# Gate products in the value tiles' PSUM banks, the value blended at eviction, and the first heads of two attentions under the value projection, in a six-layer transformer kernel

## The reference, cut to what matters

```
# layers 0 and 3 (rwkv7_time_mix)
r, k, v = xm[0] @ Wr, xm[1] @ Wk, xm[2] @ Wv
a = sigmoid(a0 + (xa @ a1) @ a2)
g = sigmoid(xg @ g1) @ g2                       # the gate
if layer == 3:                                  # the value is blended with layer 0's
    v = v + (v_first - v) * sigmoid(v0 + (xv @ v1) @ v2)
kk = normalised per head (k * k_k)
bonus = sum over a head (r * k * r_k) * v
y = scan over the tokens (r, w, k, v, kk, a)
out = ((group norm of y) + bonus) * g @ Wo
# layer 1 (stick_breaking_attention)
z = q k^T;  att = exp(log_sigmoid(z) + sum over later keys of log_sigmoid(-z));  o = att v
# layer 2 (dsa_attention)
p = softmax(q k^T / 8 over the selected keys);  o = p v
```

## Time and profile before

| what | value |
|---|---|
| three timed runs | 3889.07, 3891.84, 3902.7 us; median 3891.84 us |
| the profiled execution, its own time | 3902.21 us |
| its span, first to last instruction | 3899.5 us |
| mean granted TensorE clock | 0.982 |
| PE busy | 3746.3 us (96%) |
| POOL busy | 2632.9 us (68%) |
| ACT busy | 1880.2 us (48%) |
| DVE busy | 1612.5 us (41%) |
| transfers | 664.96 MB, mean 171 GB/s |

### The profile page before, as it was taken

One profiled execution on the slowest core, in us unless ns is written; L12 is line 12 of the kernel. 1 busy time (PEld: TensorE's weight loads), 2 busy tenths in 40 slices (PEclk: granted clock), 3 DMA queues, 4 the chain that ended last, 5 costly groups with the idle time before them and its releaser, 6 DMA issues.

```text
span 3899.5 us, 93426 instructions
## 1 busy us (share of the span) xinstructions
PE 3746.3 (96%) x36101; PEld 3562.0 (91%) x36101; DVE 1612.5 (41%) x3486; ACT 1880.2 (48%) x2746; POOL 2632.9 (68%) x1186
## 2 busy tenths in 40 slices
PE   8998998999899899899999999999999999999998
PEld 7778997998699767799999999999999999999998
DVE  6544315325532654434222375653223222266442
ACT  5325446543554432444555555455555555555643
POOL 5006873885278500288888878768888888886886
PEclk9999999998999989999999999999999999999999
DMA  6555652664356436466666646546666666664664
GB/s 186 196 202 143 183 172 76 179 184 130 87 160 191 132 112 209 146 184 189 195 193 192 191 143 186 162 136 199 191 190 194 188 186 201 185 194 129 185 182 141
DMA packets 1162954, 664.96 MB, mean 171 GB/s; under 512 B 30158, under 2 KB 1122202, under 8 KB 1162552
## 3 DMA queue, kind: packets, MB, share of 16 engines
q1 hardware_dynamic: 1162679, 661.06, 57.4%
HBM read 659.92 MB, written 1.05 MB: 170 GB/s over the span
## 4 chain that ended last, share of the span: by engine, by line
PE 43%; issue 31%; POOL 21%; DVE 3%; ACT 1%; DMA 1%; POOLq 1%; SPq 0%; DVEq 0%; ACTq 0%
PE bank L861 41%; POOL wlo L621 21%; PE bank L840 1%; DVE bank L3029 1%; POOLq L620 0%; POOLq L101 0%; ACT whi L631 0%; DMA raw<-in_w_in 0%; PE bank L961 0%; PE bank L2670 0%; PE bank L1062 0%; DVE W L1964 0%; DMA raw<-in_rw_w_rkv 0%; DVE W L1977 0%; DVE W L1962 0%
## 5 line engine op out<-in xcount | busy, mean ns | idle before, releaser
L621 POOL TENSOR_TENSOR wlo<-raw,whi 128x1024 fp32r<-128x1024 f32 (+3 forms) x1182 | 2632.7, 2245 | 1242.7 <-ACT whi L631 1238.2
L631 ACT ACTIVATE whi<-raw 128x1024 fp32r<-128x1024 f32 (+3 forms) x1182 | 1171.0, 995 | 1091.1 <-PE bank L861 915.8
L861 PE MATMUL bank<-AH,whi 128*128 128x256 f32 (+1 forms) x5712 | 1602.4, 281 | 27.4 <-DVE AL L771 9.9
L861 PE MATMUL bank<-AL,whi 128*128 128x256 f32 x5712 | 1595.1, 279 | 0.0
L861 PE MATMUL bank<-AH,wlo 128*128 128x256 f32 (+1 forms) x5712 | 1594.4, 279 | 0.0
L861 PEld LDWEIGHTS bank<-AH,whi 128*128 128x128 f32 x5712 | 1085.8, 190 | 36.4 <-issue 23.4
L861 PEld LDWEIGHTS bank<-AH,wlo 128*128 128x128 f32 x5712 | 1081.4, 189 | 0.0
L861 PEld LDWEIGHTS bank<-AL,whi 128*128 128x128 f32 x5712 | 1080.4, 189 | 0.6
L861 PE MATMUL bank<-HH,whi 128*128 128x256 f32 x1936 | 539.5, 279 | 0.0
L861 PE MATMUL bank<-HL,whi 128*128 128x256 f32 x1936 | 537.4, 278 | 0.0
L861 PE MATMUL bank<-HH,wlo 128*128 128x256 f32 x1936 | 537.4, 278 | 0.0
(11 more groups left out here) (449 smaller groups left out, 4913.6 us busy)
## 6 DMA issues: line engine op xcount, KB each, us to landing
raw<-in_ffn_w SPq DMA_DIRECT2D x420, 512.0 KB, 4.0
raw<-in_w_in SPq DMA_DIRECT2D x182, 512.0 KB, 3.9
raw<-in_ffn_w_gu SPq DMA_DIRECT2D x176, 512.0 KB, 3.8
ada_raw<-in_w_ada SPq DMA_DIRECT2D x96, 512.0 KB, 6.0
raw<-in_ffn_w_down SPq DMA_DIRECT2D x64, 512.0 KB, 3.8
raw<-in_rw_w_rkv SPq DMA_DIRECT2D x48, 512.0 KB, 3.8
raw<-in_w_ada SPq DMA_DIRECT2D x48, 512.0 KB, 5.6
raw<-in_ffn_w SPq DMA_DIRECT2D x56, 384.0 KB, 3.5
```

The lines of the kernel that those rows point to most:

```text
L621: pool.tensor_tensor(wlo[slot][:, 0:n], raw[slot][:, 0:n], whi[slot][:, 0:n], ALU.subtract).then_inc(lo_ready, 1)
L631: act.activation(whi[slot][:, 0:n], raw[slot][:, 0:n], ACT.Copy).then_inc(hi_ready, 1)
L861: mm = pe.matmul(ps[:, 0:o.shape[2]], w, o[:, k0 + c, :], start=tile not in started and c == n == 0, stop=last_panel and c == nk - 1 and n ...
```

## The change

Time mix, both layers:
- The gate products use banks 1 to 3 (`lora_banks`), the value tiles' own, in place of 4 to 7. PE no longer waits for `bonus_ready` before them but before the scan.
- The bonus product r k r_k is made on DVE right after the squares' sums, before value tile 2, and into `RW_B` (free by then), not `RW_T`. PE's bonus sums stand between value tiles 5 and 6, not behind tile 7.
- In layer 3 the value is blended as each tile is evicted (three operations of 128 x 256), and the three operations over the whole value go. Its gate (part `v`) must then be there before tile 0 is evicted. On PE its outer product stands behind value tile 0, not ahead of it.

Attentions: the first pair of heads (scores, ACT's and DVE's steps on them) is put between value tiles: after the second of four steps in `sb.v`, after the third of four in `ds.v`.

```diff
+        def lora_banks(name):
+            return bank[1:4] if name == "g" else bank[4:8]
+
         def pe_lora_out(pe, part, act_known=False):
             name = part[0]
+            banks = lora_banks(name)
...
-                if t >= 4:
+                if t >= len(banks):
                     pe.wait_ge(lora_taken, after(pe, lora_taken))
-                o, cols = bank[4 + t % 4][:, 0:S], slice(t * P, (t + 1) * P)
+                o, cols = banks[t % len(banks)][:, 0:S], slice(t * P, (t + 1) * P)
...
             if layer:
-                pe_lora(pe, parts[2])
+                pe_lora_in(pe, parts[2])
             tile(0)
+            if layer:
+                pe_lora_out(pe, parts[2])
             pe_lora_in(pe, parts[-1])
             tile(1)
...
             pe_heads(pe, const("headones"), RW_B, ready=keys_ready)
-            for s in range(2, C):
+            for s in range(2, 6):
                 tile(s)
-            pe_heads(pe, const("headones"), RW_T)
+            pe_heads(pe, const("headones"), RW_B)
+            for s in range(6, C):
+                tile(s)
             ada_round = pe_ada_start(pe, layer)
             for rnd in range(ADA_FIRST):
                 ada_round(rnd)
-            pe.wait_ge(bonus_ready, after(pe, bonus_ready))
             pe_lora_out(pe, parts[-1], act_known=True)
             pe_ada_turn(pe, bank[0], ADA_FIRST)
-            pe.wait_ge(lora_taken, after(pe, lora_taken, 4))
+            pe.wait_ge(lora_taken, after(pe, lora_taken, 3))
+            pe.wait_ge(bonus_ready, after(pe, bonus_ready))
             pe_scan(pe, layer)
...
+            def blended_value(s, j, banks):
+                o, first, ps = V[:, s * S:(s + 1) * S], VF[:, s * S:(s + 1) * S], banks[0][:, 0:S]
+                dve.tensor_tensor(o, first, ps, ALU.subtract).then_inc(dve_step, 1)
+                dve.wait_ge(dve_step, after(dve, dve_step))
+                dve.tensor_tensor(o, o, RW_XA[:, s * S:(s + 1) * S], ALU.mult).then_inc(dve_step, 1)
+                dve.wait_ge(dve_step, after(dve, dve_step))
+                dve.tensor_tensor(o, ps, o, ALU.add).then_inc(bank_free, 1)
+
+            tile = dve_tiles(dve, f"rw{layer}.v", blended_value if layer else take_copy(dve, V), by_hand=True)
+            dve.wait_ge(lora_taken, after(dve, lora_taken, 24 if layer else 16))
             tile(0)
-            dve.wait_ge(lora_taken, after(dve, lora_taken, 16))
...
+            for c in range(C):
+                cs = slice(c * S, (c + 1) * S)
+                op = dve.scalar_tensor_tensor(b[:, cs], RW_R[:, cs], vec("rw_r_k", j, c), RW_K[:, cs], ALU.mult, ALU.mult)
+            op.then_inc(head_in, 1)
+            dve.wait_ge(head_in, after(dve, head_in))
             tile(2)
             tile(3)
+            tile(4)
             dve.wait_ge(root_ready, after(dve, root_ready))
             dve.tensor_tensor(kk[:, :], kk[:, :], t[:, :], ALU.mult).then_inc(dve_step, 1)
             dve.wait_ge(dve_step, after(dve, dve_step))
-            tile(4)
...
             tile(5)
+            dve.wait_ge(head_sums, counts.at(dve, head_sums) + C // 2)
             dve.tensor_tensor(b[:, :], kk[:, :], RW_A[:, :], ALU.mult).then_inc(dve_step, 1)
...
-            if layer:
-                dve.wait_ge(head_sums, counts.at(dve, head_sums) + C // 2)
-                dve.wait_ge(lora_taken, after(dve, lora_taken, 8))
-                dve.tensor_tensor(t[:, :], VF[:, :], V[:, :], ALU.subtract).then_inc(dve_step, 1)
...
# pe_sb
+            tile = pe_panels(pe, "sb.v", fills=0, by_hand=True)
+            for st in range(G["sb.v"].steps):
+                tile(st)
+                if st == 1:
+                    pe.wait_ge(bank_free, tiles_of("sb.k"))
+                    for hd in pairs[0]:
+                        scores(hd)
             for g, pair_ in enumerate(pairs):
+                if g == 0:
+                    for hd in pair_:
+                        later(hd)
+                    pe.wait_ge(bank_free, tiles_of("sb.v"))
...
# act_sb and dve_sb: softplus(pairs[0]) and masked(hd) of the same pair behind tile(1) of sb.v
# pe_ds
+                if st == 2:
+                    pe.wait_ge(head_in, after(pe, head_in))
+                    scores(0)
+                    scores(1)
# act_ds
+                if st == 2:
+                    powers(0)
+                    powers(1)
# dve_ds
+                elif st == 2:
+                    logits(0)
+                    logits(1)
+                    weights(0)
+                    weights(1)
```

More of the change, by code:

```diff
@@ L1266, in act_lora_out @@
             dst = {"w": RW_CUM, "a": RW_A, "v": RW_XA, "g": RW_G}[name]
+            banks = lora_banks(name)
             for t in range(C):
                 act.wait_ge(lora_out, after(act, lora_out))
-                o, i = dst[:, t * S:(t + 1) * S], bank[4 + t % 4][:, 0:S]
+                o, i = dst[:, t * S:(t + 1) * S], banks[t % len(banks)][:, 0:S]
                 if name == "g":
@@ L1911, in pe_sb @@
                     pe.wait_ge(logit_ready, after(pe, logit_ready, 2))
-                for hd in pair_:
-                    later(hd)
                 if g:
+                    for hd in pair_:
+                        later(hd)
                     for hd in pairs[g - 1]:
@@ L1924, in act_sb @@
             act_norm(act, X, W[0])
-            for n in "qkv":
+            for n in "qk":
                 act_panels(act, f"sb.{n}")
@@ L1939, in softplus @@
                     act.activation(SB_SP[hd % 4], SB_SP[hd % 4], ACT.Ln, bias=1.0).then_inc(exps_ready, 1)
-            softplus(pairs[0])
+            tile = act_panels(act, "sb.v", by_hand=True)
+            for st in range(G["sb.v"].steps):
+                tile(st)
+                if st == 1:
+                    softplus(pairs[0])
             for g, pair_ in enumerate(pairs):
@@ L1989, in dve_sb @@
             pairs = [(hd, hd + 1) for hd in range(0, H, 2)]
-            for hd in pairs[0]:
-                masked(hd)
+            tile = dve_tiles(dve, "sb.v", take_tokens(dve, VT_[:, :].rearrange("p (a m) -> p a m", m=D)), by_hand=True)
+            for st in range(G["sb.v"].steps):
+                tile(st)
+                if st == 1:
+                    for hd in pairs[0]:
+                        masked(hd)
             for g, pair_ in enumerate(pairs):
@@ L2082, in pe_ds @@
                     square_sums(DS_SQ["q"])
-            tile = pe_panels(pe, "ds.v", fills=0, by_hand=True)
-            for st in range(G["ds.v"].steps):
-                tile(st)
-                if st == 0:
-                    pe_heads(pe, const("rot_head"), DS_SINE["k"])
-                if st == 1:
-                    square_sums(DS_SQ["k"])
-            pe.wait_ge(head_in, after(pe, head_in))
-            pe.wait_ge(bank_free, tiles_of("ds.v"))
             def scores(hd):
@@ L2100, in scores @@
                 mm.then_inc(ds_z_ready, 1)
+            tile = pe_panels(pe, "ds.v", fills=0, by_hand=True)
+            for st in range(G["ds.v"].steps):
+                tile(st)
+                if st == 0:
+                    pe_heads(pe, const("rot_head"), DS_SINE["k"])
+                if st == 1:
+                    square_sums(DS_SQ["k"])
+                if st == 2:
+                    pe.wait_ge(head_in, after(pe, head_in))
+                    scores(0)
+                    scores(1)
+            pe.wait_ge(bank_free, tiles_of("ds.v"))
             def turn(hd):
@@ L2169, in act_ds @@
                     inverse_norms()
-            tile = act_panels(act, "ds.v", by_hand=True)
-            for st in range(G["ds.v"].steps):
-                tile(st)
-                if st == 1:
-                    inverse_norms()
             def powers(hd):
@@ L2183, in powers @@
                 op.then_inc(exps_ready, 1)
+            tile = act_panels(act, "ds.v", by_hand=True)
+            for st in range(G["ds.v"].steps):
+                tile(st)
+                if st == 1:
+                    inverse_norms()
+                if st == 2:
+                    powers(0)
+                    powers(1)
             def turned(hd):
@@ L2303, in dve_ds @@
             normed(DS_Q)
-            tile = dve_tiles(dve, "ds.v", take_tokens(dve, DS_V[:, :].rearrange("p (a m) -> p a m", m=D)), by_hand=True)
-            for st in range(G["ds.v"].steps):
-                tile(st)
-                if st == 0:
-                    rotated(DS_K)
-                elif st == 1:
-                    normed(DS_K)
             def logits(hd):
@@ L2336, in weights @@
                 dve.wait_ge(att_ready, after(dve, att_ready))
+            tile = dve_tiles(dve, "ds.v", take_tokens(dve, DS_V[:, :].rearrange("p (a m) -> p a m", m=D)), by_hand=True)
+            for st in range(G["ds.v"].steps):
+                tile(st)
+                if st == 0:
+                    rotated(DS_K)
+                elif st == 1:
+                    normed(DS_K)
+                elif st == 2:
[3 more added lines that the diff above has]
```

(6 more changed lines are left out.)

21 lines of the change are left out of this document (1 added, 20 removed).

## The result

The kernel before takes 3891.84 us (median of 13 executions, 3881.72 to 3902.70), the changed one 3868.86 us (median of 13, 3860.63 to 3883.08): ratio 0.9942, 95% interval 0.9928 to 0.9956. It is 0.58% faster, 23 us. The forecast was 3886.3 us and "same", by which it meant within 0.5%, with a range that began at 3870. The time lies 1 us outside the range; 0.58% is past 0.5%, but the interval (0.44 to 0.72%) holds 0.5% too.

A forecast was written before the change was run, and what follows sets the result against it. Taking PE's own time as the bound, it summed -11.5 us for the attentions and -4.4 for layers 0 and 3 with one clock fall: -15.9 from 3902.21, so 3886.3 us; range 3870 to 3901.

The forecast's parts named there:

- Does the clock fall?: Before layers 0 and 3's gate products: fall 55 to 60 in 100 each, costing layer 0 12.3 us in all.
- The waits for round 1's panels: Before the gate products: 2 to 3 us of waiting for transfers, cut in pieces by thin products, in both layers.
- the pause behind tile 7: PE's wait before the direct product: 0.5 us in layer 0, 1.6 us in layer 3.
- none falls: Clock stays up in layers 0 and 3: -27.2 us in all, 3875.0 us, chance 0.20.
- The base: The sum started from the profiled execution's 3902.21 us, 10.4 above the median, as much as layer 3's low clock costs.
- the case taken: Clock falls in just one of layers 0 and 3: -15.9 us in all, 3886.3 us, chance 0.42.
- Layer 0, +1.0 forecast: Gate products start at 133.3 instead of 132.29, since round 1's panels are issued later: 1.0 us lost.
- Layer 3, -16.7 forecast: Gate products start 6.3 us earlier; with the clock up they and the scan's start save 10.4 us more.
- The value's gate product around tile 0: Layer 3: full tile 0 between its two thin halves saves 2.9 us, bounds 0 and -3.4.
- The 2.0 us at the scan's start: Layer 3: the low clock's cost in the scan's first stretch, saved if the clock is up.
- Stick-breaking attention, -3.2 forecast: First pair's softplus goes under value tiles; ACT starts the second pair at 618.3, not 621.55: 3.2 us gained.
- Sparse attention, -8.3 forecast: Head 2's logits start 3.4 us earlier, and a clock that stays up gives 4.9 us more.

The follow-up runs named there:

- e4: Kernel before with only the change's part in recurrent layers 0 and 3: ratio 0.9983 to the kernel before.
- e6: Kernel before with, of the recurrent layers' part, only the bonus sums moved behind value tile 5 and their product before tile 2: ratio 0.9968.
- e8: Whole change, but with the bonus sums behind tile 7 again, their product still made before tile 2: ratio 0.9944 to the kernel before.
- e12: Whole change timed a third time, no further edit: ratio 0.9952 to the kernel before, median 3873.26 us.
- e1: Kernel before, unchanged, timed against itself: ratio 1.0012.
- e2: Kernel before with only the stick-breaking attention's part of the change: ratio 0.9996 to the kernel before.
- e3: Kernel before with only the sparse attention's part of the change: ratio 0.9995 to the kernel before.
- e7: Kernel before with only the blend at eviction, value's gate product around tile 0 and the gate's banks; bonus sums stay behind tile 7: ratio 0.9973.
- e10: e8 with DVE taking value tiles 2 and 3 out ahead of the product for the bonus sums: ratio 0.9917 to the kernel before, median 3857.76 us.
- e9: Whole change, but with the sparse attention's first two heads' weights made behind tile 3's eviction: ratio 0.9952 to the kernel before, median 3873.17 us.
- e5: Whole change timed again, no further edit: ratio 0.9958 to the kernel before.

## Why the prediction was wrong

**What failed is the step "Does the clock fall?", in layer 3.** The prediction gave a fall 55 to 60 in 100, from the sizes of the pauses and the thin products between them. In nine profiles with no pause before the bonus sums, or one of 0.6 to 1.0 us (after, e4 to e6, e8 to e12) layer 3's gate products took 10.9 to 11.0 us; in five with one of 2.2 to 3.2 us (before, e1, e2, e3, e7) 16.2 to 19.5. The pause before the gate products went together with that one in e6, and e7 alone shows that the fall comes without it. What lies elsewhere did little: behind the 3.06 us before the direct product its first half took 5.32 us for 3.63, so the clock fell there too, but it was back by the second half (3.60) and stayed up through the gate products. The waits for round 1's panels, from which the prediction expected the fall, did not even come in layer 3 (round 1 took its 3.60 us without one), and where they came there, in e6, they made no fall. The prediction weighed the new waits for panels and the pause behind tile 7 as if any pause near the gate products did the same as the old one.

The Trainium skill's "TensorE: Matmul & The Clock Gate", section "HAM oscillation — how this bites in real kernels", says that waits for transfers between short bursts of matmuls, of some 3 to 5 us in its kernel, bring the half rate each time. Layer 3's waits for DVE, of 2.2 to 3.2 us, did so each time here. Round 1's waits for transfers, of 0.3 us, did not in e6, and layer 0's wait for DVE of 2.25 us did in two profiles (e2, e7) of the five that have it. So the length of the pause does not decide alone. Why the fall behind the old pause returns at the gate products and the one behind the new pause doesn't stays open. The nearest runs are e7 against e8 and e10, in which PE has the same work in the same order from tile 7 to the gate products: with 3.16 us before the bonus sums the clock fell in the gate products, with 2.40 before tile 6 or 1.46 before the direct product it did not. No run changed the length of a pause alone.

In layer 0 the clock is a matter of the execution. With the new order it fell in the gate products in two of six profiles (e4, e12), which cost 4.3 and 3.2 us up to the scan, where 12.3 were forecast with 2.0 of them in the scan. It also fell there in e7 and e8, which have no wait for panels in layer 0, so those waits are not shown to be the cause. So "none falls", at 0.20, was the likeliest case by the profiles, and the case of the profile after.

**The base was the wrong execution.** The sum was made against 3902.21 us, 10.4 above the median, and the prediction explained that distance by layer 3's low clock, "the faster runs may simply not have had it". That is not borne out: each of the four profiles with the old code in layers 0 and 3 shows it, e3's, of an execution of 3883.4 us, among them. The spacing of matmuls, which no step of the change touches, is large enough for the distance (43.5 us in this profile, 24 to 57 in all), but no profile of an execution near the median shows that it was this. In the later groups the kernel before had medians of 3902.7, 3897.6 and 3890.3 us, so part of it may be the chip.

The miss of 17.4 us (3886.3 less 3868.9) is then 10.4 for the base, 11.3 for the case taken (-15.9 and not -27.2), less 4.2 by which the 23.0 us measured stay under 27.2.

**Term by term.** The two profiles, before and after, are compared; other profiles of the same order scatter around them by 1 to 3 us.
- Layer 0, +1.0 forecast: the gate products start 0.97 us later (133.26 to 132.29), for the reason given. Counted from line 1219 it is +2.1 (67.0 to 65.0 us), since that line began 1.1 us earlier in this profile. e8 shows that the place of the bonus sums causes the waits for panels. In e12, where the clock fell, it was +5.5.
- Layer 3, -16.7 forecast with the clock up, -11.3 measured (89.6 to 78.3). The gate products gave 8.6 of the 8.4 forecast. The way to them gave 2.7 and not 6.3, for three reasons. The value's gate product around tile 0 was to give 2.9 us and gave 1.4 up to the squares' sums, and those only because the clock was low for 3.4 us and not 6.8: in e4, e7, e8, e9 and e12, where it was low for 6.8 us in the new order as well, this stretch takes as long as before (32.4 to 32.5 us for 32.2). The pause of 0.64 us before the bonus sums was not in the sum. And the pause behind tile 7 is 3.06 us and not 1.6: DVE's lateness was reckoned from the root at 1404.4, but DVE had been without a gap since the product of 5.44 us ahead of tile 2, which the prediction had hidden at no cost, and which was 2.2 us longer than before. Taking two tiles out before it gave 2.5 us back in layer 3 (e10 against e8). The 2.0 us at the scan's start don't show in its length, which is 169 to 173 us in the old order and 168 to 174 in the new.
- Stick-breaking attention, -3.2 forecast, -3.5 measured (80.9 to 77.4).
- Sparse attention, -8.3 forecast, -5.7 measured (93.9 to 88.2), and 3 to 6 over the other profiles (92.1 to 92.5 before, 86.6 to 89.1 with the whole change). PE's pause at the third head's scores was to be 1.3 us (1014.1 to 1015.4). It is 2.26 and 2.32 us in two profiles of the whole change and 1.15 in e12, and each time as long, within 0.01 us, as DVE's two small operations (L2342) ahead of tile 3's eviction took together. The clock fell all the same in all three, for 3.4 us (e5) to 14 (e12, behind the shortest pause). With a pause of 1.03 us and no fall, in e10, the stage took 83.9 us, 8.5 less: the forecast for a clock that stays up.
- The sum of these is +2.1 - 11.3 - 3.5 - 5.7 = -18.4 us. The levelled ends of the two profiles say -18.9, the averages of three and two profiles -20, the three timings -23 (-28 to -17), -16 and -17. But the sum agrees in part by luck. The two scans took 5.6 us more in the profile after than before (1.2 and 4.4), and the kernel behind layer 3's scan, which the change doesn't touch, took less. Levelled as above, that stretch takes 2249 to 2253 us in the seven profiles with the whole change in them (after, e5, e8 to e12) and 2255 to 2260 in the seven others, on the same chip too (e5 and e8 against e6 and e7). So some 6 us of the gain come from code that is the same in both kernels, and only with the parts together (e2, e3 and e4 don't have it): theory B in kind, though not the 10 to 20 us that it named. Some 4 of them stand around two waits of PE for DVE, at 2257 and 2496 us in the kernel before. What shortens them no run shows.

## What to carry over

Before the sum is made against one profile, ask where that execution stands among the timed ones and whether its surplus lies in stages that the change touches; if not, take it off. A low clock behind a pause that is at the same place in every execution can be worth more than the pause itself (8.6 us behind 2.2 here), and e6 got it back with the bonus sums' place alone. Work that is moved earlier on an engine with slack is not free if evictions are queued behind it, or if another engine's work falls on it there: e10 got 2.5 us back in layer 3 by taking two evictions first. And before two profiles of different edits are subtracted, compare them ahead of the edit: 1.7 us of e10's 4.2 lay there.

## What the hardware showed unexpectedly

Matmuls of 128x256 that follow each other without a wait come 113 or 117 to 118 ns apart at a granted clock of 1.00. The level lasts for tens to hundreds of microseconds and differs between executions of the same code at the same place (342 and 355 in 40 us). Over the kernel it makes 24 to 57 us, more than the whole change. That it makes the spread of some 30 us between executions is likely from its size but not shown: in the three profiles of the whole change it makes 24.0 to 35.0 us, and their last matmuls start within 1.3 us of each other. What sets it no run here shows.

Some operations of DVE take 0.5 to 2.2 us more than their like, and end with a subtraction of POOL's (L621). The one on 128 x 2 elements ahead of PE's wait in the sparse attention takes 0.17 us at its shortest. In the kernel before it took

```profile
1015.93 1.48 DVE L2323 TENSOR_SCALAR top<-top 128x2 f32<-128x2 f32 x1
```

and ended at 1017.41, POOL's subtraction at 1017.38. In the profile after these are 993.41 and 993.38. Over the six profiles with the old order there (before, e1, e2, e4, e6, e7) this operation took 0.73 to 1.89 us, and PE's pause behind it was in each 1.5 us longer than the operation. In the kernel before 29 operations of DVE are longer than the median of their line by over 0.6 us, 45.8 us in all, and 24 of them end no more than their usual length after one of POOL's subtractions. In the profiles it looks as if DVE waited for POOL there; no run isolates it.
